# Recurrence of a hybrid encoder layer: streams and X on GpSimd's DMA queue, decay sums at the end of the period, keys turned in their own period, v staged in TK and W

## The reference, cut to what matters

```python
def rwkv7_scan(r, w, k, v, kk, a, reverse):
    def step(state, inp):
        r_t, w_t, k_t, v_t, kk_t, a_t = inp
        sa = jnp.einsum('bhvk,bhk->bhv', state, kk_t)
        state = (state * w_t[:, :, None, :]
                 - sa[..., None] * (kk_t * a_t)[:, :, None, :]
                 + v_t[..., None] * k_t[:, :, None, :])
        return state, jnp.einsum('bhvk,bhk->bhv', state, r_t)
    ...
y = (rwkv7_scan(r_h, decay_h[0], k_dir[0], v_h, kk, a_h[0], reverse=False)
     + rwkv7_scan(r_h, decay_h[1], k_dir[1], v_h, kk, a_h[1], reverse=True))
```

## Time and profile before

| | us |
|---|---|
| time, median of 3 runs | 1704.05 (1703.67 to 1710.66) |
| the profiled execution, its own time | 1705.89 |
| its span in the profile | 1703.9 |
| recurrence in it: PE's first `cumulate` to its last `sum_y` | 223.65 to 621.5 |
| first `fill` of units 0 to 7 | 305.12, 352.31, 387.65, 430.13, 473.47, 516.79, 557.57, 589.13 |
| experts: first gather to the end | 729.9 to 1703.9 |

### The profile page before, as it was taken

How to read it: one execution, slowest core, us unless ns; L and a number is a source line. 1 busy time by engine, 2 the same in 40 slices (tenths; PEclk the granted TensorE clock), 3 DMA queues, 4 the chain that set the end, 5 groups by cost and what they waited for, 6 DMA issues and landing times.

```text
span 1703.9 us, 26170 instructions
## 1 busy us (share of the span) xinstructions
PE 1487.5 (87%) x11264; PEld 743.3 (44%) x11264; DVE 526.3 (31%) x725; ACT 257.4 (15%) x487; POOL 198.6 (12%) x358
## 2 busy tenths in 40 slices
PE   5999978787777779589999899899898998998996
PEld 2444444687777655343333333333333432433332
DVE  8756523466555365401101101110110111111012
ACT  2333311112111112110010010100100100100101
POOL 6122503233333311000000000000000000000000
PEclk7999988899899899789999999999999999999999
DMA  8144583644555654559999999999999999999995
GB/s 256 62 148 155 175 275 54 166 106 114 120 125 125 150 199 194 197 209 410 413 415 413 412 415 414 410 415 415 411 413 415 413 412 415 414 411 415 415 411 237
DMA packets 239963, 500.22 MB, mean 294 GB/s; under 512 B 131056, under 2 KB 140272, under 8 KB 223504
## 3 DMA queue, kind: packets, MB, share of 16 engines
q1 hardware_dynamic: 234112, 479.29, 75.5%
q0 software_dynamic: 5776, 19.82, 3.4%
HBM read 470.76 MB, written 28.31 MB: 293 GB/s over the span
## 4 chain that ended last, share of the span: by engine, by line
PE 33%; SPq 10%; DMA 10%; ACT 1%; issue 1%; DVE 1%; DVEq 0%; ACTq 0%
SPq L1134 10%; DMA ring<-in_exp_w_down 10%; PE pG L1480 9%; PE pU L1480 8%; PE pD L1499 6%; PE pO L1526 5%; PE pX L1462 4%; PE pX L1487 1%; ACT xin L1540 1%; ACT yexp L1555 0%; PE pX L1507 0%; DVE pick L1581 0%; DVE res L1612 0%; ACT hidT L1552 0%; ACT xin L1564 0%
## 5 line engine op out<-in xcount | busy, mean ns | idle before, releaser
L1480 PE MATMUL pU<-ring,xin 128*64 128x512 f32 x1024 | 226.8, 595 | 0.0
L1499 PE MATMUL pD<-ring,hidT 128*64 128x512 f32 x768 | 171.0, 595 | 18.6 <-ACT hidT L1552 11.3
L1600 DVE TENSOR_TENSOR res<-res,pO 128x512 f32<-128x512 f32 x128 | 88.0, 687 | 321.1 <-PE pO L1526 321.1
L1595 DVE TENSOR_TENSOR hid<-silu,pU 128x512 f32<-128x512 f32 x32 | 22.0, 687 | 518.2 <-PE pU L1480 518.2
L1526 PE MATMUL pO<-yexp,scatter 128*128 128x512 f32 x256 | 123.2, 618 | 20.2 <-ACT yexp L1555 20.2
L1480 PEld LDWEIGHTS pU<-ring,xin 128*64 128x64 f32 x1024 | 70.7, 137 | 132.5 <-issue 130.6
L1480 PE MATMUL pG<-ring,xin 128*64 128x512 f32 x512 | 114.8, 595 | 11.0 <-ACT xin L1540 11.0
L1480 PE MATMUL pG<-lent_slot,xin 128*64 128x512 f32 x512 | 113.0, 594 | 0.0
L1499 PEld LDWEIGHTS pD<-ring,hidT 128*64 128x64 f32 x768 | 54.2, 137 | 122.9 <-issue 96.2
L1526 PEld LDWEIGHTS pO<-yexp,scatter 128*128 128x128 f32 x256 | 39.4, 188 | 104.8 <-DVE res L1600 62.9
L1462 PE MATMUL pX<-pick,y 128*128 128x128 f32 x512 | 63.2, 283 | 14.2 <-DVE pick L1581 14.2
(11 more groups left out here) (222 smaller groups left out, 1741.8 us busy)
## 6 DMA issues: line engine op xcount, KB each, us to landing
ring<-in_exp_w_up SPq DMA_DIRECT2D x64, 2048.0 KB, 24.0
ring<-in_exp_w_down SPq DMA_DIRECT2D x48, 2048.0 KB, 21.4
ring<-in_exp_w_gate SPq DMA_DIRECT2D x32, 2048.0 KB, 23.6
lent_slot<-in_exp_w_gate SPq DMA_DIRECT2D x32, 2048.0 KB, 24.1
lent_slot<-in_exp_w_down SPq DMA_DIRECT2D x16, 2048.0 KB, 23.8
lent_slot<-in_rw_w_in SPq DMA_DIRECT2D x8, 1024.0 KB, 12.6
scratch_sw<-tok POOLq DMA_DIRECT2D x8, 512.0 KB, 3.8
scratch_bz<-bz POOLq DMA_DIRECT2D x16, 256.0 KB, 3.7
```

The costliest lines, as they stand in the source:

```text
L1480: mm = pe.matmul(psum[HEAD * s:HEAD * s + HEAD, :], xin[:, k, e, :], w[:, k, HALF * s:HALF * s + HALF], start=k == 0, stop=k == DC - 1)
L1499: mm = pe.matmul(pD[h][HEAD * s:HEAD * s + HEAD, :], hidT[:, j, c, HEAD * s:HEAD * s + HEAD], w[:, 4 * half + 2 * s + c % 2, HALF * h:HALF ...
L1595: dve.tensor_tensor(hid[:, j, :], silu[:, :], pU[:, :], ALU.mult).then_inc(hid_done, 1)
L1600: dve.tensor_tensor(cols, cols, pO[h][:, :], ALU.add).then_inc(scat_add, 1)
```

## The change

- **Queues.** The four streams of a unit are loaded by POOL (`load_streams` takes an engine), behind `base` and the X part of the inverses of the unit before the last. `send_inverses(eng, n, a, dst)` now does one half of what `inverses` did: SP does a = 0 (XT), POOL a = 1 (X), each with its own write, wait and two reads, and `base_out` and `base_in` are a pair of semaphores each. SP keeps the decays, v, the blocks and XT. `load_decays(n + 3)` moves ahead of `inverses(n + 1)` and waits until PE has summed the decays of unit n+2.
- **Decay sums.** `cumulate(n + 3, (0, 1))` moves to the end of period n, between the two `sum_y`; `cumulate(n + 2, (2, 3))` stands between the first two fills.
- **Keys.** `turn_keys(n)` moves from the end of period n-1 into period n, two parts behind each pair of second-step fills. ACT's copy moves with it.
- **DVE's order.** Both `queries(n + 2)` go ahead of the first `add_to`, the keys behind; one semaphore `prep_done` replaces the two. `masked(n + 2, 1)` to `masked(n + 2, 3)` move one place forward each, and so do `scores(n + 2, 1)` to `scores(n + 2, 3)` on PE.
- **Start.** v is staged in TK (tiles 0, 1 and 3) and W (tile 2), each tile with its own semaphore, so v of unit 0 is loaded right after `blocks(0)`, and `blocks(1)` no longer stands behind the last v. X is zeroed by ACT.

```diff
-        v_stage = [UV[k][:, :, :, :, :].rearrange("p e c u v -> p (e c u v)")[:, 0:D] for k in range(2)]
+        tk_flat = TK[:, :, :, :].rearrange("p c u s -> p (c u s)")
+        v_stage = [tk_flat[:, 0:HALF], tk_flat[:, HALF:D], W[:, :, :].rearrange("p k s -> p (k s)"), tk_flat[:, D:2 * D]]
...
+        def load_streams(eng, n):
+            t, b = tile(n), n % 2
+            for s, src in ((R_, scr["r"][t]), (KK_, scr["kk"][t]), (BZ_, scr["bz"][b, t]), (KD_, scr["kd"][b, t])):
+                eng.dma_start(IN[:, s, :], src.rearrange("p c s -> p (c s)")).then_inc(streams_in, 16)
+
+        def send_inverses(eng, n, a, dst):
+
+            if n:
+                eng.wait_ge(base_in[a], 32 * n)
+            eng.dma_start(diagonal("inverses", a), XB[:, a]).then_inc(base_out[a], 16)
+            eng.wait_ge(base_out[a], 16 * (n + 1))
+            if a == 0 and n >= 2:
+                eng.wait_ge(u_mm, 2 * (n - 1))
+            if a == 1 and n:
+                eng.wait_ge(inv_mm, FILLS * (n - 1) + 8)
+            for e in range(2):
+                eng.dma_start(dst[rows(e), :, :], square("inverses", a, e)).then_inc(base_in[a], 16)
...
             def load_decays(n):
+                sp.wait_ge(cum_mm, 4 * n)
                 sp.dma_start(IN[:, SW_, :], scr["sw"][n % 2, tile(n)]).then_inc(decays_in, 16)
...
             load_w_v(1)
-            load_streams(0)
             load_w_v(0)
...
             blocks(0)
+            load_v(0)
+            load_decays(2)
             sp.wait_ge(zeroed, 64)
             inverses(0)
...
+            sp.wait_ge(v_ev, V_SECOND + 1)
+            sp.dma_start(scr["v"][2], v_stage[2]).then_inc(v_out[2], 16)
             blocks(1)
...
                 load_v(n + 1)
+                if n + 3 < UNITS:
+                    load_decays(n + 3)
                 inverses(n + 1)
-                if n + 3 < UNITS:
-                    sp.wait_ge(prep_dve, n + 3)
-                    sp.wait_ge(prep_keys, n + 3)
-                    load_decays(n + 3)
-                    load_streams(n + 3)
                 if n + 2 < UNITS:
                     blocks(n + 2)
...
         def _(pool):
+            load_streams(pool, 0)
...
+            pool.wait_ge(prep_done, 1)
+            load_streams(pool, 1)
             for n in range(UNITS):
                 base(n)
+                if n == 0:
+                    pool.wait_ge(zeroed, 64)
+                send_inverses(pool, n, 1, X)
+                if n + 2 < UNITS:
+                    pool.wait_ge(prep_done, n + 2)
+                    load_streams(pool, n + 2)
...
                 fill(n, 0, 0, scored(n), of(X))
                 if ahead:
-                    cumulate(n + 2, (0, 1))
+                    cumulate(n + 2, (2, 3))
                 fill(n, 1, 1, scored(n), of(X))
...
                     fill(n, g, g, of(W), of(XT[n % 2]))
+                    turn_keys(n, (2 * g, 2 * g + 1))
...
                 sum_y_state(n, 1)
+                if ahead:
+                    scores(n + 2, 1)
                 solve_u(n, 1)
                 if ahead:
-                    scores(n + 2, 1)
+                    scores(n + 2, 2)
...
                 if ahead:
                     sum_state(n, 1)
-                    scores(n + 2, 2)
+                    scores(n + 2, 3)
                 sum_y(n, 0)
-                if ahead:
-                    scores(n + 2, 3)
-                if n < LAST:
-                    turn_keys(n + 1, (0, 1))
+                if n + 3 < UNITS:
+                    cumulate(n + 3, (0, 1))
                 sum_y(n, 1)
-                if n < LAST:
-                    turn_keys(n + 1, (2, 3))
```

On DVE the loop becomes:

```diff
                 for g in range(2):
                     cross(n, 0, g, g, 1 + g)
                 if ahead:
-                    removed_keys(n + 2, 0)
+                    for k in range(2):
+                        queries(n + 2, k)
...
                     add_to(n, XT[n % 2], g, g, 4 + 2 * g)
+                if ahead:
+                    removed_keys(n + 2, 0)
                 for g in range(2):
                     cross(n, 1, g, 2 + g, 7 + g)
-                if ahead:
-                    removed_keys(n + 2, 1)
...
                 if ahead:
-                    added_keys(n + 2, 0)
+                    removed_keys(n + 2, 1)
                 removed(n, 0)
                 if ahead:
-                    queries(n + 2, 0)
+                    added_keys(n + 2, 0)
                 add_state(n, 0)
                 if ahead:
                     added_keys(n + 2, 1)
-                    queries(n + 2, 1)
                     masked(n + 2, 0)
+                    masked(n + 2, 1)
                 removed(n, 1)
                 if ahead:
-                    masked(n + 2, 1)
+                    masked(n + 2, 2)
                     add_state(n, 1)
-                    masked(n + 2, 2)
+                    masked(n + 2, 3)
                 add_y(n, 0)
-                if ahead:
-                    masked(n + 2, 3)
                 add_y(n, 1)
```

More of the change, by code:

```diff
@@ L614, in inverses @@
                 sp.wait_ge(base_done, n + 1)
-                if n:
-                    sp.wait_ge(base_in, 64 * n)
-                for a in range(2):
-                    sp.dma_start(diagonal("inverses", a), XB[:, a]).then_inc(base_out, 16)
-                sp.wait_ge(base_out, 32 * (n + 1))
-                if n >= 2:
-                    sp.wait_ge(u_mm, 2 * (n - 1))
-                if n:
-                    sp.wait_ge(inv_mm, FILLS * (n - 1) + 8)
-                for a, dst in enumerate((XT[n % 2], X)):
-                    for e in range(2):
-                        sp.dma_start(dst[rows(e), :, :], square("inverses", a, e)).then_inc(base_in, 16)
+                send_inverses(sp, n, 0, XT[n % 2])
             def load_w_v(h):
@@ L700, in base @@
                 if n:
-                    pool.wait_ge(base_out, 32 * n)
+                    for a in range(2):
+                        pool.wait_ge(base_out[a], 16 * n)
                 link(pool.tensor_copy(XB[:, 0].rearrange("p s t -> p (s t)"), con[:, C_EYE:C_EYE + BASE * BASE]))
@@ L720, in _, with zero_x @@
         def _(act):
+            def zero_x():
+                act.activation(X[:, :, :].rearrange("p k s -> p (k s)"), con[:, 0:D], ACT.Copy, scale=0.0).then_inc(x_cleared, 1)
             def decays(n):
@@ L754, in projected @@
                     t, h = V_PIECES[k]
[L755 to L756 removed]
                     act.wait_ge(v_mm, k + 1)
[L758 removed]
+                    at = HALF * h if t >= 2 else 0
+                    act.activation(v_stage[t][:, at:at + HALF], pT[k % 2][:, :], ACT.Copy).then_inc(v_ev, 1)
+            zero_x()
             decays(0)
@@ L767, in _ @@
                     decays(n + 2)
+                if n == 0:
+                    for t in (0, 1, 3):
+                        act.wait_ge(v_out[t], 16)
+                turned_keys(n)
                 negated_r(n, 0)
@@ L908, in _ @@
             project_v((V_SECOND + 1,))
-            turn_keys(0, range(4))
-            pe.wait_ge(cleared, 3)
+            cumulate(2, (0, 1))
+            pe.wait_ge(cleared, 2)
             pe.wait_ge(v_ev, len(V_PIECES))
@@ L913, in _ @@
                 ahead = n + 2 < UNITS
-                pe.wait_ge(base_in, 64 * (n + 1))
+                for a in range(2):
+                    pe.wait_ge(base_in[a], 32 * (n + 1))
                 if n:
@@ L926, in _ @@
                 sum_r(n, 0)
-                if ahead:
-                    cumulate(n + 2, (2, 3))
                 for g in range(2):
@@ L1049, in prep @@
             def prep(n):
+                for k in range(2):
+                    queries(n, k)
                 for e in range(2):
                     removed_keys(n, e)
+                for e in range(2):
                     added_keys(n, e)
-                for k in range(2):
-                    queries(n, k)
             for n in range(2):
```

91 lines of the change are left out of this document (34 added, 57 removed).

## The result

The changed kernel takes 1689.22 us (median of 5 runs, 1687.62 to 1694.22) where the kernel before took 1708.38 on the same chip (5 runs, 1703.67 to 1710.66): a ratio of 0.9899, 95% interval 0.9874 to 0.9923. Run again later it took 1690.30 against 1706.08, 0.9915 (0.9883 to 0.9947). So the change is faster by 16 to 19 us, about half of the 37 forecast, and its time lies above the range, which ended at 1686. The profiled execution has a span of 1688.1 and an own time of 1690.05; the forecast on that basis was 1668.9, so 21.2 are to be found.

What follows compares the result with a forecast made beforehand. It took the serial turn of SP's list, which brings X to PE, to bound the recurrence at 43.3 us a period. (31.5 + 39.7) / 2 gives 35.6; 39.0 us won, less 2, makes 1667 us; range from 1650 to 1686.

Steps and rivals of the forecast that it cites:

- The two limits: In the recurrence, PE's own period and the way of one unit's inverse over two periods; the later one sets each unit's start.
- T7: Start of PE's first fill of unit 7; forecast 550.1, against 589.1 before the change.
- T1: Start of PE's first fill of unit 1; forecast 342.0.
- d: Offset in its period at which a unit's last mask ends; 31.5 us forecast, 31.8 with SP's wake of 0.3.
- L: Way of a unit from its last mask over blocks, NB, `base`, write and X to its first fill; 39.7 us.
- The blocks: Time from the last mask's release on SP until the blocks have landed and NB is issued; 7.5 us, ends 4.8 and 10.5.
- rival B: The queues share the DMA engines, so the blocks keep their 10.5 us; time 1676, chance 0.15.
- X: Reads of X by POOL beside SP's for XT, until the unit's first fill; 6.6 us, between 6.0 and 8.6.
- P: PE's own period in the recurrence, without waits for X; 33.6 us, from 35.3 before.
- rival D: POOL's queue is slow for short runs, a few ns a run; 1720 at 5 ns, chance 0.06 for slower.
- Rival E: Streams land 4 us later, so DVE holds PE by some 3 us in five periods; time 1682, chance 0.06.
- Rival C: PE bounds all periods, as X comes early and the start costs nothing; time 1650, chance 0.1.

Runs made afterwards that it cites:

- e5: Changed kernel with the streams from unit 3 on issued by SP in two pairs, behind the NB load and behind v and decays, under `base`: 1673.44 us.
- e3: Changed kernel with the streams of units 3 to 7 issued by SP, behind XT and ahead of the blocks, X still on POOL: 1699.51 us.
- e11: e5 with XB, XT and X back on SP, so POOL issues nothing from unit 3 on: 1678.10 us.
- e4: Changed kernel with XB, XT, X and the streams of units 3 to 7 all on SP again, its start and orders kept: 1701.45 us.
- e8: e7 with each stream of units 3 to 7 cut into two DMAs with 512-byte runs instead of 4 KB: 1699.03 us.
- e7: Changed kernel with the streams of units 3 to 7 issued by ACT once POOL's write of XB has landed, in 4 KB runs: 1700.53 us.
- e2: Changed kernel with the streams of units 3 to 7 not loaded, so those units compute with stale streams: 1668.51 us.
- e9: e6 with period 7 reordered: ACT squares y ahead of `negated_r` and its copies of turned keys, PE turns those keys later: 1662.85 us.
- e6: e5 with X by SP and XT by POOL, PE waiting for XT only at the first fill that reads it: 1671.00 us.

## Why the prediction was right or wrong

**The two limits and the form of the sum** were right. T7 = T1 + 3 (d + L) - 5.5 gives 571.1 with the measured 78.4, and 3 x 7.2 = 21.6, with 2.7 from period 7 and less the 2 taken off in advance, makes 22.3; T1 is 0.5 earlier than forecast and the part behind the first gate matmul 0.5 shorter, which leaves the 21.2 that are missing. That T1 fits is luck in part: an early T0 and an unforeseen wait for X cancel.

**The blocks, the term that failed.** "I take 7.5 and keep both ends" rested on "in flight again while the blocks go, but side by side". Side by side was not better than one behind the other: 12.2 to 14.3, beyond the high end of 10.5. The row of that end was read as the price of standing behind the streams in a queue. It was the price of sharing the engines with them: SP had then spent 3.4 on issuing decays and streams first, so that the engines had a start on them. In the changed kernel the blocks leave between 1.0 ahead of the first stream and 0.9 behind it, so the argument against rival B, that "the blocks start while the streams are half through", was wrong as well. The bundle kept its length (from the issue of XT 17.5 to 18.0 before, 16.1 to 16.7 after with 512 KB less in it), so the less of the streams is through when the blocks start, the longer is their own term, and the length of the bundle was the quantity to predict. Rival B named the mechanism and was given 0.15; with 10.5 it too was mild, for its 1676 is passed by 13. It was e5 against e3 and e11 against e4 that showed it. The rule that stood beside rival B holds here for the blocks: the Trainium skill, DMA: Bandwidth & Descriptors, section "Issuing engines are not separate DMA queues"; the trace and the runs agree, with 12.2 for the blocks of the change, 13.7 in e8 and 4.84 in e5 on one queue. It does not tell the 6 to 11 us by which e3 and e7 lie above the changed kernel: there X took longer.

**X** was 7.7 where 6.6 was taken, inside its ends; the blocks and the streams run beside it (5.7 in the median in e5). **d** was 32.6 with the wake, where 31.8 was forecast: the first instructions after a wait are slow (1.42 and up to 1.97 for the 32 matmuls of the first fill, 1.15 otherwise, and 2.09 for the 8 of the `cumulate` behind it, 1.16 otherwise). In period 1, whose first fill takes 1.15, d is 31.7. PE stands 3.51 for X ahead of 421.36; the granted clock is 0.81 and 0.82 in the windows from 419 to 428, so a part of them ran at the lower level of 1.2 GHz, and 1.00 (2.4 GHz) from 428 to 446. This second cost of a wait for X was in the sum once, in the 2 taken off, and not in each period.

**Period 7** failed in its sentence "the turned keys in it lie under the head norm". They lie ahead of it: PE turns them before `sum_r_state`, ACT's `negated_r` waits for that, and the squares of the head norm stand behind `negated_r`. That costs 2.3 of the 2.7; the rest is in slower fills.

**Right**: P (33.6; e2 has 33.9 and 33.4 for T3 to T4 and T4 to T5). The start: T0 306.2 and T1 341.5, the projection at 235.75. `base` 15.5. POOL's queue: XB took 1.23 to issue, X 1.65 for two and a stream 0.54 to 0.57, where 1.5, 2.0 and 0.56 were worked out, so rival D fell; the write and wait were 5.8, between the ends. Rival E did not come either: the last stream lands 9.9 after its issue, 9.3 in the earlier trace rows; `queries` starts 5.1 to 6.7 after Tn and waits for kd twice, 1.07 and 0.57. That is past the 6 at which the prediction saw the cover end, but no wait of PE over 0.6 follows it. Rival C was right on P and wrong on L: it needs the streams out of the way, and even e2 and e9, which have that, stay 18 and 13 above its 1650. The engines beside each other: POOL's rows for its DMAs stay at 0.54 to 1.65 while DVE works on two SBUF inputs, on the side of the row that the prediction followed.

**What stays open**: how the engines share their turns between transfers; and whether X's place is the whole of the 6 to 11 us that the streams cost more on SP's or ACT's queue. A run with the streams on SP, issued 1.6 behind POOL's reads of X, would tell.

## What to carry to other kernels

A second queue gives back the time of issuing, not that of the transfer. Before moving a load to another queue, read the busy share of the DMA engines by stretches: if the stretch is full, predict the length of the whole bundle, and take each short transfer in it as landing near its end. A large load belongs in the stretch where the engines idle, here behind the short load that releases `base`, and there one queue was nearly as good as two. Look also at the other transfers in the stretch for which an engine waits: here X took some 3 us longer when the streams came from another queue than its own. A step that is moved into the last period has to be looked at there by itself, on each engine that it uses.

## What of the hardware was not expected

- A short transfer can be slower beside a large one than behind it: the 512 KB of blocks took 4.85 alone, 10.5 behind the streams in one queue, 12.2 to 14.3 beside them on two. Leaving 1.0 ahead of the streams on a queue of their own did not help them: 14.1.
- Cutting the streams' runs from 4 KB to 512 bytes changed nothing that could be measured (1700.53 and 1699.03).
- A DMA of POOL was ready later than one of SP that was issued with it: of the two halves of XB, issued at 485.82 by SP and 486.09 by POOL, the one was ready at 490.18, the other at 491.58. In e6, which swaps the halves, SP's is again the earlier: issued at 434.04 and 434.30, ready at 437.09 and 439.19. POOL's issue takes 1.2, SP's 0.4, so 0.8 to 0.9 of the later readiness, 1.1 and 1.8, is in the issue.
- POOL's issue time grew with the number of runs, but slowly: 0.55 for 128 runs, 0.82 for 1024, 1.23 for 2048.
